# Second FFN of a diffusion backbone on one Trainium2 core: the norm applied to the results of the first products

## The reference, cut to what matters

```python
hx = rms_norm(x, norm_ffn[i]) * (1.0 + mod_x[4]) + mod_x[3]
x = x + mod_x[5] * ((jax.nn.silu(hx @ w1) * (hx @ w3)) @ w2)
# rms_norm(x, g) = x * rsqrt(mean(x * x) + 1e-6) * g
```

## Time and profile before

| what | us |
|---|---|
| median of 3 runs (lowest, highest) | 1246.41 (1242.51, 1246.7) |
| the profiled execution, its own time | 1245.67 |
| its span in the profile | 1243.9 |
| PE busy in the span | 1162.7 (93%) |
| DVE busy | 879.7 (71%) |
| ACT busy | 591.6 (48%) |
| POOL busy | 223.3 (18%) |

### The profile page before, as it was taken

One profiled execution on the slowest core, in us unless ns is written; L12 is line 12 of the kernel. 1 busy time (PEld: TensorE's weight loads), 2 busy tenths in 40 slices (PEclk: granted clock), 3 DMA queues, 4 the chain that ended last, 5 costly groups with the idle time before them and its releaser, 6 DMA issues.

```text
span 1243.9 us, 19284 instructions
## 1 busy us (share of the span) xinstructions
PE 1162.7 (93%) x6954; PEld 974.1 (78%) x6954; DVE 879.7 (71%) x1311; ACT 591.6 (48%) x984; POOL 223.3 (18%) x166
## 2 busy tenths in 40 slices
PE   5799999898999999999999889999999897999997
PEld 3577776678988888878888778887677797999996
DVE  0896888975887777774665688888999666555453
ACT  3647888733532323232222556446466445666442
POOL 0201444422100000000111100005877211000010
PEclk9899999999999999989999999999999898999999
DMA  9543222240575555554552142221221343655562
GB/s 380 190 129 126 61 93 86 69 170 1 189 240 171 186 194 202 178 187 142 161 162 68 58 122 81 86 84 50 70 68 55 116 153 115 192 180 189 150 186 71
DMA packets 48176, 168.23 MB, mean 135 GB/s; under 512 B 5233, under 2 KB 6513, under 8 KB 47857
## 3 DMA queue, kind: packets, MB, share of 16 engines
q1 hardware_dynamic: 48112, 167.38, 40.4%
HBM read 166.31 MB, written 1.05 MB: 135 GB/s over the span
## 4 chain that ended last, share of the span: by engine, by line
PE 69%; DVE 17%; ACT 7%; issue 4%; DMA 1%; SPq 1%; POOL 1%; DVEq 0%; ACTq 0%
PE bank L1666 20%; PE bank L1668 20%; PE bank L1667 20%; DVE scratch L1442 5%; DVE w_lo L1073 3%; PE bank L2091 2%; ACT w_hi L607 2%; DMA raw<-in_w_in 1%; ACT scratch L912 1%; PE bank L2103 1%; DVE softmax_max L1244 1%; PE bank L2124 1%; ACT conv_in L909 1%; PE bank L2113 1%; DVE mla_h_lo L1264 1%
## 5 line engine op out<-in xcount | busy, mean ns | idle before, releaser
L1073 DVE TENSOR_TENSOR w_lo<-raw,w_hi 128x1024 fp32r<-128x1024 f32 (+1 forms) x226 | 281.4, 1247 | 158.7 <-ACT w_hi L607 158.5
L607 ACT ACTIVATE w_hi<-raw 128x1024 fp32r<-128x1024 f32 (+1 forms) x226 | 230.8, 1023 | 274.0 <-PE bank L1668 252.0
L1666 PE MATMUL bank<-ffn_h_lo,w_hi 128*128 128x256 f32 (+1 forms) x736 | 246.0, 334 | 8.9 <-DVE ffn_h_lo L1110 5.6
L1667 PE MATMUL bank<-ffn_h_hi,w_hi 128*128 128x256 f32 (+1 forms) x736 | 245.3, 333 | 0.0
L1668 PE MATMUL bank<-ffn_h_hi,w_lo 128*128 128x256 f32 (+1 forms) x736 | 245.2, 333 | 0.0
L1666 PEld LDWEIGHTS bank<-ffn_h_lo,w_hi 128*128 128x128 f32 x736 | 140.4, 191 | 24.3 <-issue 6.0
L1668 PEld LDWEIGHTS bank<-ffn_h_hi,w_lo 128*128 128x128 f32 x736 | 140.4, 191 | 14.6
L1667 PEld LDWEIGHTS bank<-ffn_h_hi,w_hi 128*128 128x128 f32 x736 | 140.5, 191 | 14.4
L462 POOL TENSOR_TENSOR scratch<-scratch 128x512 f32<-128x512 f32 (+1 forms) x24 | 34.6, 1443 | 618.8 <-ACT scratch L616 618.8
L1666 PE MATMUL bank<-ffn_hidden_lo,w_hi 128*128 128x256 f32 (+1 forms) x374 | 125.0, 334 | 5.8 <-DVE ffn_hidden_lo L1402 5.8
L1666 PE MATMUL bank<-ssd_h_lo,w_hi 128*128 128x256 f32 (+2 forms) x360 | 125.3, 348 | 5.0 <-DVE ssd_h_lo L1347 2.3
(11 more groups left out here) (264 smaller groups left out, 2147.0 us busy)
## 6 DMA issues: line engine op xcount, KB each, us to landing
raw<-in_w SPq DMA_DIRECT2D x120, 512.0 KB, 4.3
scratch<-in_vec_w SPq DMA_DIRECT2D x56, 512.0 KB, 3.6
vec_weights<-in_vec_w SPq DMA_DIRECT2D x24, 512.0 KB, 3.6
raw<-in_w_xbc SPq DMA_DIRECT2D x24, 512.0 KB, 3.5
ada_start<-in_ada_w SPq DMA_DIRECT2D x8, 1024.0 KB, 17.2
raw<-in_w_z SPq DMA_DIRECT2D x16, 512.0 KB, 3.5
raw<-in_w_so SPq DMA_DIRECT2D x16, 512.0 KB, 3.6
raw<-in_w SPq DMA_DIRECT2D x16, 384.0 KB, 3.8
```

Source lines behind the costliest of these rows:

```text
L607: A(wh[s % RING][:, 0:c], raw[s % RING][:, 0:c], ACT.Copy).then_inc(w_hi, 1)
L1073: V.tensor_tensor(wl[s % RING][:, 0:c], raw[s % RING][:, 0:c], wh[s % RING][:, 0:c].bitcast(f32), SUB).then_inc(w_lo, 1)
L1666: mm(o, lh, rl, start=first, stop=False)
L1667: mm(o, lh, rh, start=False, stop=False)
```

## The change

The factor 1/rms of a token is the same for all features, so it can be taken out of the product: w1 applied to (x * gain) / rms + shift is (w1 applied to x * gain) / rms + w1 applied to shift. The new kernel does this for w1 and w3 of the second FFN.

- H2h and H2l now hold X times gain, without 1/rms, and two more columns with the shift (latent and context; only the first is used later). They are written as soon as a tile of X is final: `gained_hi` on ScalarE, `gained_lo` on VectorE, between the steps of the output tiles. GpSimd's part in it is gone.
- Every product of w1 and w3 has 258 moving columns instead of 256. Column 256 of the result is the weight applied to the shift.
- TensorE runs the first w1 tile ahead of `norm_sum`, waiting for each k of H2l; then `norm_sum`, then the other tiles, each after the one before it.
- VectorE multiplies each result by 1/rms on its way out of the bank and copies column 256 to `shift_out`. ScalarE's SiLU reads that from `scratch` and adds the shift's column as its bias. VectorE adds the other shift in the multiplication that follows.

```diff
@@ buffers, semaphores, GpSimd @@
-            H2h, H2l = (sb(f"ffn1_h_{p}", [128, KD, LAT], f32r, ph) for p in ("hi", "lo"))
+            H2h, H2l = (sb(f"ffn1_h_{p}", [128, KD, LAT + 2], f32r, ph) for p in ("hi", "lo"))
+            shift_out = sb("shift_out", [128, 2, 2], f32, ph)
...
+        h2_hi, h2_lo, f1_scaled, f3_scaled = sem("gained_hi"), sem("gained_lo"), sem("first_scaled"), sem("third_scaled")
...
             accumulate(6, LAT)
-            over_rms(6, lambda k: X[:, k, CTX:TOK], CTX, TOK)
             accumulate(7, LAT)
@@ ScalarE @@
             rms(5, LAT, INNER)
-            xlat = [(0, CTX, TOK)]
+            act.wait_ge(hy_lo, KI)
+            A(H2h[:, :, LAT:LAT + 2], mod[1][:, 24:32, :], ACT.Copy).then_inc(h2_hi, 1)
+            def gained_hi(m):
+                act.wait_ge(added, ADD2 + m + 1)
+                A(H2h[:, m, 0:LAT], X[:, m, CTX:TOK], ACT.Copy, scale=gain[3][:, m, 0:1]).then_inc(h2_hi, 1)
+            gained_hi(0)
             squares(6, 0, ADD2, CTX)
             for m in range(1, 8):
...
+                gained_hi(m)
                 squares(6, m, ADD2, CTX)
             hi(SO + 19, SO + 19)
             rms(6, LAT, D)
-            his_shared(6, xlat, lambda k, c0, c1: H2h[:, k, :], lambda k, m: gain[3][:, k, m:m + 1], lambda k, m: mod[1][:, 24 + k, m:m + 1])
+            def hidden_scaled(j, g, u, n, s):
+                hi(n + 4, s + 4)
+                act.wait_ge(f1_scaled, 2 * j + 2)
+                act.wait_ge(hid_f, g - 1)
+                A(T[:, u, 0:LAT], T[:, 6 + u, 0:LAT], ACT.Silu, bias=shift_out[:, u, 0:1]).then_inc(silu_done, 1)
+                hi(n + 5, s + 5)
+                act.wait_ge(hid_f, g + 1)
+                A(U1h[:, ds(j, 1), :].rearrange("p o t -> p (o t)"), T[:, 2 + u, 0:LAT], ACT.Copy).then_inc(hid_hi, 1)
             with act.Fori(0, KH // 2) as i:
                 for u in range(2):
-                    hidden(2 * i + u, KH + 2 * i + u, u, LAT, U1h, F1 + 4 * i + 2 * u, F1 + 2 * u)
+                    hidden_scaled(2 * i + u, KH + 2 * i + u, u, F1 + 4 * i + 2 * u, F1 + 2 * u)
@@ VectorE @@
+            dve.wait_ge(h2_hi, 1)
+            V.tensor_tensor(H2l[:, :, LAT:LAT + 2], mod[1][:, 24:32, :], H2h[:, :, LAT:LAT + 2].bitcast(f32), SUB).then_inc(h2_lo, 1)
+            def gained_lo(m):
+                dve.wait_ge(h2_hi, m + 2)
+                V.scalar_tensor_tensor(H2l[:, m, 0:LAT], X[:, m, CTX:TOK], gain[3][:, m, 0:1], H2h[:, m, 0:LAT].bitcast(f32),
+                                       MUL, SUB).then_inc(h2_lo, 1)
             for m in range(8):
                 scale_add(m)
+                if m:
+                    gained_lo(m - 1)
...
+            gained_lo(7)
             lo(SO + 19, SO + 19)
-            dve.wait_ge(added, ADD3)
-            norm(6, lambda k, c0, c1: X[:, k, c0:c1], 8, xlat, lambda k, m: gain[3][:, k, m:m + 1],
-                 lambda k, c0, c1: H2h[:, k, :], lambda k, c0, c1: H2l[:, k, :], lambda k, m: mod[1][:, 24 + k, m:m + 1])
+            inverse_root(6, LAT)
+            dve.wait_ge(inv, DONE[6] + 1)
+            def hidden_scaled(j, g, u, n, s):
+                dve.wait_ge(w_used, n + 1)
+                dve.wait_ge(silu_done, g - 1)
+                V.tensor_tensor(T[:, 6 + u, 0:LAT], bank[2 + 2 * u][:, 0:LAT], T[:, 5, 0:LAT], MUL).then_inc(f1_scaled, 1)
+                V.tensor_copy(shift_out[:, u, 0:1], bank[2 + 2 * u][:, LAT:LAT + 1]).then_inc(f1_scaled, 1)
+                lo(n + 4, s + 4)
+                dve.wait_ge(w_used, n + 2)
+                dve.wait_ge(hid_lo, g - 1)
+                V.tensor_tensor(T[:, 2 + u, 0:LAT], bank[3 + 2 * u][:, 0:LAT], T[:, 5, 0:LAT], MUL).then_inc(f3_scaled, 1)
+                V.tensor_copy(shift_out[:, u, 1:2], bank[3 + 2 * u][:, LAT:LAT + 1]).then_inc(f3_scaled, 1)
+                lo(n + 5, s + 5)
+                dve.wait_ge(f3_scaled, 2 * j + 2)
+                dve.wait_ge(silu_done, g + 1)
+                V.scalar_tensor_tensor(T[:, 2 + u, 0:LAT], T[:, 2 + u, 0:LAT], shift_out[:, u, 1:2], T[:, u, 0:LAT], ADD, MUL).then_inc(hid_f, 1)
+                dve.wait_ge(hid_hi, g + 1)
+                V.tensor_tensor(U1l[:, ds(j, 1), :].rearrange("p o t -> p (o t)"), T[:, 2 + u, 0:LAT],
+                                U1h[:, ds(j, 1), :].rearrange("p o t -> p (o t)").bitcast(f32), SUB).then_inc(hid_lo, 1)
@@ TensorE @@
-            norm_sum(6, LAT)
-            h2 = (lambda k: H2h[:, k, :]), (lambda k: H2l[:, k, :])
+            def gained_tile(n, s, o, first):
+                pe.wait_ge(w_lo, n + 1)
+                for k in range(KD):
+                    if first:
+                        pe.wait_ge(h2_lo, k + 2)
+                    w = slice(128 * k, 128 * k + 128)
+                    last = three(o[:, 0:LAT + 2], wh[s % RING][:, w], wl[s % RING][:, w], H2h[:, k, :], H2l[:, k, :], k == 0, k == KD - 1)
+                last.then_inc(w_used, 1)
             for j in range(2):
-                ffn(j, KH + j, j, LAT, *h2, F1 + 2 * j, F1 + 2 * j, NB[6] if j == 0 else None)
+                gained_tile(F1 + 2 * j, F1 + 2 * j, bank[2 + 2 * j], j == 0)
+                if j == 0:
+                    norm_sum(6, LAT)
+                gained_tile(F1 + 2 * j + 1, F1 + 2 * j + 1, bank[3 + 2 * j], False)
             with pe.Fori(1, KH // 2) as i:
                 for u in range(2):
-                    ffn(2 * i + u, KH + 2 * i + u, u, LAT, *h2, F1 + 4 * i + 2 * u, F1 + 2 * u, None)
+                    pe.wait_ge(f1_scaled, 4 * i + 2 * u - 2)
+                    gained_tile(F1 + 4 * i + 2 * u, F1 + 2 * u, bank[2 + 2 * u], False)
+                    pe.wait_ge(f3_scaled, 4 * i + 2 * u - 2)
+                    gained_tile(F1 + 4 * i + 2 * u + 1, F1 + 2 * u + 1, bank[3 + 2 * u], False)
```

More of the change, by code:

```diff
@@ L1638, in _ @@
                     lo(SO + 18, SO + 18)
+            gained_lo(7)
             lo(SO + 19, SO + 19)
-            dve.wait_ge(added, ADD3)
-            norm(6, lambda k, c0, c1: X[:, k, c0:c1], 8, xlat, lambda k, m: gain[3][:, k, m:m + 1],
-                 lambda k, c0, c1: H2h[:, k, :], lambda k, c0, c1: H2l[:, k, :], lambda k, m: mod[1][:, 24 + k, m:m + 1])
+            inverse_root(6, LAT)
[17 more added lines that the diff above has]
+                                U1h[:, ds(j, 1), :].rearrange("p o t -> p (o t)").bitcast(f32), SUB).then_inc(hid_lo, 1)
             with dve.Fori(0, KH // 2) as i:
                 for u in range(2):
-                    hidden(2 * i + u, KH + 2 * i + u, u, LAT, U1h, U1l, F1 + 4 * i + 2 * u, F1 + 2 * u)
+                    hidden_scaled(2 * i + u, KH + 2 * i + u, u, F1 + 4 * i + 2 * u, F1 + 2 * u)
             for m in range(8):
```

## The result

| | us |
|---|---|
| median after, 8 runs (lowest, highest) | 1251.53 (1248.84, 1253.43) |
| median before, 8 runs beside them | 1246.56 (1242.2, 1248.27) |
| ratio | 1.0046, 95% interval [1.0032, 1.0061] |
| profiled execution after, its own time and span | 1248.84, 1247.1 |

A forecast was written before the change was run, and what follows sets the result against it. TensorE was taken to pace the FFN before the change; afterwards a ScalarE-VectorE ring would start w2 0.4 us later, plus 0.9 for slower products, sum +1.2, so 1246.9 us. Its own range was 1243 to 1251.

The forecast's parts named there:

- The front's chain: Additions to X ahead of the FFN: ScalarE's gained copy adds four steps of 0.40 us, last addition 1.6 us later.
- Sum, root, first scaling: Behind the first tile: sum out at 1036.3, root at 1036.8, reciprocal 1.75 us, VectorE's first scaling at 1038.65.
- TensorE at its upper level, waiting in the first tile: First w1 tile: starts at 1030.3 with granted clock 1.00 right through, waits some 1.5 us inside the tile.
- The ring: FFN loop: ScalarE and VectorE steps waiting on each other take 12.0 us a turn (7.3 plus 4.7), against TensorE's 11.45.
- TensorE hardly notices: FFN loop: ScalarE and VectorE fall behind 0.55 us a turn, but only the last turns come near delaying TensorE's blocks.
- rival B: FFN loop: dear handoffs and pointer operands, ring 12.7 us, TensorE waits in the last four turns too; 1254.2 us; chance 0.15.
- The gap: Ahead of the w2 products: TensorE idle for some 9 us, waiting for the last low part.
- The slow stretch: Behind the idle time ahead of w2: ten more products at the lower clock, 0.095 us each, 0.9 us.
- The second products "don't change": w2 products behind the loop: taken as unchanged, so given no term in the sum.
- The 258 columns: w1 and w3 products: two more columns cost 0.0009 us a product, 1.0 us in all on TensorE.
- Rival C: FFN loop: each table load holds ScalarE 2.56 us, 28 us on top, 1275; chance 0.05 together with dear columns.
- Rival A: FFN loop: ring stays under 11.45 us, TensorE bounds to the end, w2 6.1 us earlier, 1239.6 us; chance 0.16.

The follow-up runs named there:

- e2: Changed kernel with VectorE's product with the SiLU moved ahead of the low part of block n+5, both table loads kept: 1240.33 us, ratio 0.9948.
- e11: Changed kernel with a one-element square root on ScalarE between the two tiles of each turn, making four table loads a turn: 1277.71 us, ratio 1.0242.
- e5: e2 with 896 bytes a partition left free ahead of the hidden layer's tensors: 1240.6 us, ratio 0.9949.
- e6: e2 with first products of 256 columns in place of 258, layout kept: 1241.21 us, ratio 0.9954.
- e1: Changed kernel with a one-column SiLU at the head of each ScalarE turn, leaving one table load a turn: 1243.21 us, ratio 0.9967.
- e12: Kernel before, with the second products' wait for the last hidden column group moved ahead of the first tile's third block: 1241.56 us, ratio 0.9949.
- e8: Changed kernel with a one-element square root on ScalarE at the end of each turn; still two table loads a turn: 1251.05 us, ratio 1.0036.
- e10: e2 plus a reordered front stretch, with rows of 320 columns instead of 258 in the first products' operand tensors: 1239.39 us, ratio 0.9919.

## Why the prediction was right, and what in it was not

The forecast was +1.2 us on the profiled execution, by a ring that eats what the front gains. It came as +4.4 from the mark. The path and the sign were right, and the forecast that the change stays within half a per cent holds. The amount was not right: all misses but one go the same way, and the median of 1251.53 lies just above the forecast's own range, 1243 to 1251. By its steps:

- **The front's chain.** Forecast: four steps of 0.40, +1.6 on the last addition. Measured: 23.15 us from the first addition to the last, against 20.88, +2.27. The step was right (3.91 against 3.52 between the last two additions, 0.39). The count was wrong: six of the seven distances grew, by 0.29 to 0.41, since the copy stands in the chain from the second addition on. That is 0.67.
- **Sum, root, first scaling.** Forecast 5.5 us from the last addition's start to the first scaling, measured 1038.35 - 1032.63 = 5.7. Of it 0.32 is VectorE's wait for its own reciprocal. 0.2.
- **TensorE at its upper level, waiting in the first tile.** Right: granted clock 1.00. The wait was 2.39 us instead of some 1.5: 0.7 of it is the later addition again, and 0.3 that the tile started 19.36 us from the mark instead of 19.67.
- **The ring.** Forecast 12.0 a turn, 7.3 and 4.7. Measured 12.14: 7.38 from 1109.14 to 1116.52 and 4.75 to 1121.27. The terms: SiLU 0.51, next start 0.41 later (0.40 taken); column copy 0.15 (0.15); first load to next start 1.29 (1.30); rounding's end to low part 1117.10 - 1116.94 = 0.16 (0.12). From the first scaling to the second products' start it is 132.5 us against 131.0 forecast: 1.5, the largest miss, and 11 x 0.14. e2 showed that the ring is the cause, e11 its price.
- **"TensorE hardly notices."** Wrong in size. TensorE was to end the first products at 1159.3, 148.6 from the mark; it ended them at 152.0. Of these 3.3 us 2.5 are its waits for blocks in the last four turns, 0.4 the products' distance (0.1196 instead of 0.1192), 0.3 the later second tile. Waits in the last four turns were forecast for rival B alone, with a ring of 12.7; they came with 12.14. They don't move the sum, since the ring sets when w2 starts. The lag of the low part behind its w3 tile grew from 5.1 to 5.9 us at the start to 9.2 to 10.4 at the end, as forecast (5 to 6, 9 to 10), but it stopped growing where TensorE began to wait.
- **The gap.** Forecast some 9 us, measured 9.24. The agreement is luck: by the prediction's own times it is 1169.6 - 1159.3 = 10.3, and TensorE's waits in the loop took off what the longer ring put on. From the mark it is the 2.74 of before, 3.7 by which TensorE ends earlier, and 2.8 by which w2 starts later. 11 + 11 loads in the loop, as expected.
- **The slow stretch.** Forecast ten more products at the lower level and +0.9. Products more than 0.17 us apart: 17 before, 23 after. The excess is 2.3 us against 1.6, +0.7.
- **The second products "don't change".** Wrong, and the term that the sum left out without a reason: 528 of them at 0.1200 instead of 0.1183 are 0.9 us, by e5 the placement of the hidden layer's tensors.
- **The 258 columns.** The size was about right (0.0012 a product against 0.0009) for a wrong reason: not the columns, the layout (e6). It was free in the changed kernel, since the ring paced the loop, and costs 1.3 us in e2.

Together 0.67 + 0.2 + 1.5 - 0.2 + 0.9 = 3.1 on top of 1.2: 4.3 of the 4.4 measured. Rival C (twice its row for each load) is refuted by e11: two more loads and the small square root made the turn 2.67 us longer, where the doubled price would have given over 5. So on the rule of the Trainium skill (ScalarE: Activation LUTs, What ACT_TABLE_LOAD costs) the row decides: 1.28 to 1.30 us a load here, and no drain of 1.38 more. Rival A, the ring under TensorE's pace, was forecast 0.55 us a turn away and was 0.67 away (12.14 - 11.47); e2 crosses it by moving one instruction. For A the prediction had worked out a gap of 3.8 and 6.1 us less than before. e1, which keeps the changed kernel's order on VectorE, shows a gap of 3.92 and 4.4 less (228.8 against 233.2 from the mark); e2, with the product ahead of the low part, 2.74 and 5.4 less.

## What to carry to other kernels

When an operation is moved behind a matmul, list which engine waits for which in one turn of the loop, and add the ring up. What counts is neither busy shares (68% and 69% here) nor the number of instructions, but whether one turn's last step releases the next turn's first. If the ring is longer than the bound engine's turn by a few per cent, the difference is paid every turn and appears late: here as short waits for blocks in the last four of eleven turns and as one long wait behind the loop. Take independent work (here the split of a weight block) out from between two steps of the ring before anything else. Look at the waits at both ends of a loop as well: a wait for the last of many operands can be put behind work on the first ones, which took 4.5 us off the kernel before here (e12).

## What was not expected of the hardware

- The same product, 128x128 by 128x256 in float32r, starts every 0.1183 or every 0.1200 us, depending on where in SBUF its moving operand lies: 128 bytes a partition further on made the difference, and 896 more took it back (e5). Rows of 1032 bytes gave 0.1195, of 1280 bytes 0.1200, of 1024 bytes 0.1183.
- Two more columns in 256 cost nothing that the rows show (e6).
- A table load can vanish when another is added (e8): a square root at the end of the loop's body made the load ahead of the copy at its head unnecessary.
- With the same gap of 2.74 us TensorE's slow stretch held 15 to 17 wide starts in most traces but 28 in e10, 2.8 us of excess instead of 1.6. Why is open; it hides e10's gain in the second products.
